# Value stage of a hybrid trunk kernel: the gate-activations are rounded on ScalarE, and the gates lie in device memory in another order

## The reference, cut to what matters

```
q = (x @ w_q).reshape(n, P_HEADS, 2, P_QDIM // 2)
s = jnp.einsum('nhjd,hjkd->nhjk', q, sub_keys).astype(jnp.float32)
sv, si = lax.top_k(s, P_TOPK)
...
gate = jax.nn.softmax(tv, axis=-1).astype(x.dtype)
u = u_tab[eidx]
act = jax.nn.gelu(jnp.einsum('nhkd,nd->nhk', u, x), approximate=False)
return jnp.einsum('nhk,nhkd->nd', gate * act, v_tab[eidx])
```

## Time and profile before

| | us |
|---|---|
| median of 3 runs | 2930.12 |
| lowest, highest run | 2927.99, 2931.79 |
| the profiled execution | 2933.7 |
| span in its profile, first to last instruction | 2931.1 |
| first `v` tile on TensorE, layer 0 and layer 1 | 1112.1, 2459.2 |

### The profile page before, as it was taken

One profiled execution on the slowest core, in us unless ns is written; L12 is line 12 of the kernel. 1 busy time (PEld: TensorE's weight loads), 2 busy tenths in 40 slices (PEclk: granted clock), 3 DMA queues, 4 the chain that ended last, 5 costly groups with the idle time before them and its releaser, 6 DMA issues.

```text
span 2931.1 us, 51716 instructions
## 1 busy us (share of the span) xinstructions
PE 2811.6 (96%) x20358; PEld 2653.3 (91%) x20358; DVE 1930.2 (66%) x4036; ACT 1030.2 (35%) x1440; POOL 996.9 (34%) x695
## 2 busy tenths in 40 slices
PE   7989999999899999999998979999999999999998
PEld 4966558999899999999998868999899999999997
DVE  3876654587683236888886566488685324888886
ACT  4611104333353333323234354333254333233223
POOL 0000000127888722434320000107788742343430
PEclk9999999999999999999999999999999999999999
DMA  7346634777678778999993303587678778999994
GB/s 244 111 145 235 206 108 151 260 212 172 146 216 196 176 199 277 324 321 326 335 313 114 123 21 123 170 271 179 157 194 210 176 180 261 310 328 330 321 326 151
DMA packets 340184, 631.67 MB, mean 216 GB/s; under 512 B 73808, under 2 KB 221392, under 8 KB 337696
## 3 DMA queue, kind: packets, MB, share of 16 engines
q1 hardware_dynamic: 140960, 428.57, 45.4%
q0 software_dynamic: 81024, 99.92, 13.6%
q10 hardware_dynamic: 118016, 100.67, 10.8%
HBM read 533.37 MB, written 95.35 MB: 215 GB/s over the span
## 4 chain that ended last, share of the span: by engine, by line
PE 89%; DVE 5%; DMA 3%; ACT 1%; issue 1%; another core or an unknown queue 0%; ACTq 0%; SPq 0%; DVEq 0%
PE ps L1216 29%; PE ps L616 15%; PE ps L618 15%; PE ps L617 15%; DMA ring<-in_ada 2%; PE ps L1195 1%; PE ps L589 1%; DVE arena L1664 1%; PE ps L726 1%; PE ps L677 1%; DMA arena<-act_dram 1%; PE ps L1168 1%; PE ps L708 1%; PE ps L793 1%; PE ps L853 1%
## 5 line engine op out<-in xcount | busy, mean ns | idle before, releaser
L1664 DVE TENSOR_TENSOR w_lo<-ring,w_hi 128x1024 fp32r<-128x1024 f32 x576 | 702.6, 1222 | 519.4 <-ACT w_hi L1312 503.6
L1216 PE MATMUL ps<-ga_parts,w_hi 128*128 128x320 f32 x4096 | 901.7, 309 | 3.0 <-DVE ga_parts L1664 3.0
L616 PE MATMUL ps<-hT_hi,w_hi 128*128 128x384 f32 x2576 | 869.2, 337 | 9.5 <-ACT arena L1588 8.1
L617 PE MATMUL ps<-hT_lo,w_hi 128*128 128x384 f32 x2576 | 862.5, 335 | 2.4 <-issue 2.4
L618 PE MATMUL ps<-hT_hi,w_lo 128*128 128x384 f32 x2384 | 798.5, 335 | 2.0 <-issue 2.0
L1312 ACT ACTIVATE w_hi<-ring 128x1024 fp32r<-128x1024 f32 x378 | 400.1, 1060 | 960.3 <-PE ps L618 772.6
L1216 PEld LDWEIGHTS ps<-ga_parts,w_hi 128*128 128x128 f32 x4096 | 684.6, 188 | 3.8 <-issue 2.5
L1216 PE MATMUL ps<-ga_parts,w_lo 128*128 128x320 f32 x2048 | 632.2, 309 | 0.0
L616 PEld LDWEIGHTS ps<-hT_hi,w_hi 128*128 128x128 f32 x2576 | 485.0, 188 | 13.4 <-issue 12.9
L617 PEld LDWEIGHTS ps<-hT_lo,w_hi 128*128 128x128 f32 x2576 | 485.2, 188 | 3.7 <-issue 3.2
L618 PEld LDWEIGHTS ps<-hT_hi,w_lo 128*128 128x128 f32 x2384 | 448.9, 188 | 2.7 <-issue 2.7
(11 more groups left out here) (347 smaller groups left out, 2382.7 us busy)
## 6 DMA issues: line engine op xcount, KB each, us to landing
ring<-in_u SPq DMA_DIRECT2D x256, 512.0 KB
ring<-in_v SPq DMA_DIRECT2D x256, 512.0 KB
ring<-in_ada SPq DMA_DIRECT2D x96, 512.0 KB
act_dram<-arena SPq DMA_DIRECT2D x256, 192.0 KB
arena<-g_dram ACTq DMA_DIRECT2D x32, 1280.0 KB
arena<-act_dram ACTq DMA_DIRECT2D x32, 1280.0 KB
g_dram<-arena POOLq DMA_DIRECT2D x24, 1024.0 KB, 24.7
ring<-in_mix_in SPq DMA_DIRECT2D x42, 512.0 KB
```

The source lines that it names most:

```text
L616: pe.matmul(out, hi[:, c, :], hT_hi[:, c, :], start=(c == 0), stop=False)
L617: pe.matmul(out, hi[:, c, :], hT_lo[:, c, :], start=False, stop=False)
L1216: mm = pe.matmul(ps[:, c, 0:DENSE], l_[:, cs], r_, start=(first and q == 0), stop=(last and q == 2))
L1664: return dve.tensor_tensor(out, a, b, op)
```

## The change

1. VectorE no longer makes the rounded part of `ga`. ScalarE does, in the new `round_in(j, r)`: when tile j-2 is multiplied and the product of tile j is there, it copies `ga` into `ga_parts` with rounding. `round_in(0)` and `round_in(1)` stand ahead of the loop, behind the wait for `act_stored`; in the loop `round_in` of tile j+2 stands ahead of `high_in` of tile j+4.
2. `g_dram` becomes `[i, group of 8 columns, block of 16 tokens, column in the group, token in the block]`, without the first 64 tokens. One `gtile` is then 10,240 consecutive bytes for each i, where it was 20 runs of 512 B. `store_block` writes 16 runs of 512 B for each i, where it wrote 8 KB in one. Zeroing is 16 DMAs of 6 KB for each i, where it was 12 of 8 KB. The addresses for the scatter need the column number's upper and lower bits apart, which adds three operations of VectorE in each of token tiles 0 and 1 (`place_in_g`).

```diff
+DBLK = DENSE // GBLK
+G_ROW, G_JUMP = NJ * DENSE, (DENSE - GBLK) * GJ
...
-        g_dram = nc.dram_tensor("g_dram", [NBLK, P, P, GBLK], F32).ap()
+        g_dram = nc.dram_tensor("g_dram", [P, NJ // GJ, DBLK, GJ, GBLK], F32).ap()
...
                 def store_block(b, blk):
-                    act.dma_start(g_dram[blk].rearrange("i j t -> i (j t)"),
-                                  gstage[:, b].rearrange("p j t -> p (j t)")).then_inc(g_stored[b], 16)
+                    act.dma_start(g_dram[:, :, blk - GATHERED // GBLK].rearrange("i g j t -> i g (j t)"),
+                                  gstage[:, b].rearrange("p (g j) t -> p g (j t)", j=GJ)).then_inc(g_stored[b], 16)
...
-                    act.dma_start(gtile[:, b], g_dram[GATHERED // GBLK:, :, bass.ds(m * GJ, GJ), :].rearrange("b i j t -> i b (j t)"))\
+                    act.dma_start(gtile[:, b].rearrange("p b x -> p (b x)"), g_dram[:, bass.ds(m, 1)].rearrange("i g b j t -> i (g b j t)"))\
                        .then_inc(g_in[b], 16)
...
+                def round_in(j, r=0):
+
+                    act.wait_ge(multiplied, (g0 + j - 1) + r * 2 * GJ)
+                    act.wait_ge(ga_f32, (NJ * layer + j + 1) + r * 2 * GJ)
+                    act.activation(ga_parts[:, j % 2, 0:DENSE], ga[:, j % 2, :], ACT.Copy).then_inc(ga_high, 1)
+
                 for i in range(ASLOTS):
                     act.wait_ge(act_stored[i], 16 * (NJ * (layer + 1) // ASLOTS))
+                round_in(0)
+                round_in(1)
                 with act.Fori(0, NJ // (2 * GJ) - 1) as r:
                     for b in range(2):
                         for k in range(GJ):
+                            round_in(GJ * b + k + 2, r)
                             high_in(WB + GJ * b + k, r)
                         act.wait_ge(ga_f32, (NJ * layer + GJ * (b + 1)) + r * 2 * GJ)
                         load_tiles(r * 2 + (b + 2), b)
-                for j in range(NJ - 2 * GJ + WB, NJ):
-                    high(g0 + j)
+                for j in range(NJ - 2 * GJ + 2, NJ):
+                    round_in(j)
+                    if j + 2 < NJ:
+                        high(g0 + j + 2)
...
+                def place_in_g(row, col, block):
+
+                    chained(dve.tensor_copy(col_group, col))
+                    dve.tensor_scalar(row, row, float(G_ROW), float(block * GJ * GBLK), ALU.mult, ALU.add)
+                    chained(dve.tensor_scalar(col_group, col_group, 3, None, ALU.logical_shift_right))
+                    chained(dve.scalar_tensor_tensor(col, col, float(GBLK), row, ALU.mult, ALU.add))
+                    chained(dve.tensor_scalar(col, col, sc_tok[:, 3:4], None, ALU.add))
...
-                    dve.wait_ge(multiplied, (g - 1) + r * 2 * GJ)
-                    dve.wait_ge(ga_f32, (n + 1) + r * 2 * GJ)
-                    dve.tensor_copy(ga_parts[:, k % 2, 0:DENSE], ga[:, k % 2, :]).then_inc(ga_high, 1)
                     dve.wait_ge(ga_high, (n + 1) + r * 2 * GJ)
...
-                for blk in range(GATHERED // GBLK, 2 * P // GBLK):
-                    pool.dma_start(g_dram[blk].rearrange("i j t -> i (j t)").rearrange("i (r c) -> i r c", c=256), bc(zeros, 1, 8))\
+                for m in range(NJ // GJ):
+                    pool.dma_start(g_dram[:, m, 0:12].rearrange("i b j t -> i (b j t)").rearrange("i (r c) -> i r c", c=256), bc(zeros, 1, 6))\
                         .then_inc(g_zeroed, 16)
```

More of the change, by code:

```diff
@@ L2289, in rank @@
                 chained(dve.reciprocal(gsum[:, 0, :], gsum[:, 0, :]))
+                col_group = gate_rest.bitcast(U32)
+                def place_in_g(row, col, block):
[4 more added lines that the diff above has]
+                    chained(dve.tensor_scalar(col, col, sc_tok[:, 3:4], None, ALU.add))
                 if t == 1:
                     tt(whole_gate.rearrange("p k h -> p h k"), tv, bc(gsum[:, 0, :], 2, TOPK), ALU.mult)
[L2292 to L2295, removed]
+                    row, col = sel3[:, 0, :], sel3[:, 1, :]
+                    place_in_g(row, col, 4)
+                    dve.scalar_tensor_tensor(whole_at.rearrange("p k h -> p (k h)"), col_group, float(G_JUMP), col, ALU.mult, ALU.add)\
+                       .then_inc(scatter_ready, 1)
                     lows(None)
@@ L2303, in rank @@
                     chained(dve.scalar_tensor_tensor(sel3[:, 2, :], col, float(P), row, ALU.mult, ALU.add))
-                    chained(dve.scalar_tensor_tensor(row, row, float(P), col, ALU.mult, ALU.add))
-                    dve.tensor_scalar(row, row, float(GBLK), None, ALU.mult)
+                    place_in_g(row, col, -4)
                     dve.tensor_copy(at[0][near], sel3[near, 2, :])
-                    chained(dve.tensor_scalar(col, sel3[:, 2, :], float(T), None, ALU.mult))
-                    dve.tensor_scalar(at[0][far], row[far], sc_tok[far, 3:4], None, ALU.add)
-                    dve.tensor_scalar(at[1][near], col[near], sc_tok[near, 4:5], None, ALU.add).then_inc(scatter_ready, 1)
+                    dve.scalar_tensor_tensor(at[0][far], col_group[far], float(G_JUMP), col[far], ALU.mult, ALU.add)
+                    chained(dve.tensor_scalar(row, sel3[:, 2, :], float(T), None, ALU.mult))
+                    dve.tensor_scalar(at[1][near], row[near], sc_tok[near, 4:5], None, ALU.add).then_inc(scatter_ready, 1)
                     lows(None)
@@ L2370, in peer @@
                 chained(dve.tensor_scalar(low_part, number, GBLK - 1, None, ALU.bitwise_and))
-                chained(dve.scalar_tensor_tensor(sc_tok[:, 3:4], high_part, float(P * P * GBLK), low_part, ALU.mult, ALU.add))
+                chained(dve.scalar_tensor_tensor(sc_tok[:, 3:4], high_part, float(GJ * GBLK), low_part, ALU.mult, ALU.add))
                 dve.tensor_copy(iota_u, bc(iota[:, 0:LOOK], 2, P))
@@ L2496, in _ @@
                 pool.dma_start(A["out_state"][d], sfin[:, d]).then_inc(outs_done, 16)
-            g_flat = g_dram.rearrange("b i j t -> (b i j t)").unsqueeze(1)
+            g_flat = g_dram.rearrange("i g b j t -> (i g b j t)").unsqueeze(1)
             act_flat = act_dram.rearrange("j i t -> (j i t)").unsqueeze(1)
@@ L2503, in scatter_gates @@
                 pool.wait_ge(zeros_ready, layer + 1)
-                for blk in range(GATHERED // GBLK, 2 * P // GBLK):
-                    pool.dma_start(g_dram[blk].rearrange("i j t -> i (j t)").rearrange("i (r c) -> i r c", c=256), bc(zeros, 1, 8))\
+                for m in range(NJ // GJ):
+                    pool.dma_start(g_dram[:, m, 0:12].rearrange("i b j t -> i (b j t)").rearrange("i (r c) -> i r c", c=256), bc(zeros, 1, 6))\
                         .then_inc(g_zeroed, 16)
-                pool.wait_ge(g_zeroed, 16 * 12 * (layer + 1))
+                pool.wait_ge(g_zeroed, 16 * (NJ // GJ) * (layer + 1))
                 pool.wait_ge(scatter_ready, 2 * layer + 1)
```

## The result

| | before | after |
|---|---|---|
| median of 20 runs each, us | 2922.07 | 2935.70 |
| lowest, highest | 2913.78, 2934.93 | 2928.61, 2945.91 |
| ratio after to before, 95% interval | | 1.0043, 1.0032 to 1.0054 |
| the profiled execution; its span | 2933.7; 2931.1 | 2934.43; 2932.6 |

The change costs 12.6 us (9.4 to 15.8).

What follows compares the result with a forecast made beforehand. It took TensorE to bound the value stage, at 3.52 us a tile. Start +12.1, clock +4.2, gains -0.8 and -1.2, end +0.4 made +14.7 us on 2930.1: 2944.8 us, own range 2937 to 2951, with rivals 2925 to 2962.

Steps and rivals of the forecast that it cites:

- The start: Start of each layer's value stage: TensorE waits while the first rounding stands behind the gelu store's landing, 6.3 and 5.8 us, +12.1.
- The clock: After the pause at each value stage's start TensorE resumes at half clock: twice 2.1, +4.2 us, bounds 0 and 6.8.
- The gains: Shorter second load issue no longer delays a gelu in the `u` stage, -0.8 us; late load at tile 32 in time, -1.2.
- The end: Gap ahead of the last two tiles grows by ScalarE's longer rounding and a hand-over, 0.2 us a layer: +0.4 us.
- The sum: All terms together: 12.1 + 4.2 - 0.8 - 1.2 + 0.4 = +14.7 us.
- Steady state: Value loop: rounding on ScalarE lengthens the chain by 0.2 us, within 2.4 us of slack a tile; cost zero.
- First rival: Value loop: the second load's issue stays slow because of its own 1,024 runs; 33 us excess, 2978 us; chance 0.13.
- Second rival: Scatter phase: changed addresses end TensorE's holes in both layers, 19.5 us come back, 2925 us; chance 0.12.
- Third rival: `u` stage: `gstage` stores in 512 B runs take 10.1 us each instead of 3.3; 2971 to 3025 us; chance 0.07.

Runs made afterwards that it cites:

- e1: The changed kernel with both first roundings ahead of ScalarE's wait for the stored gelus: 2916.97 us, ratio 1.0017 to the kernel before.
- e2: The changed kernel with tile 0's rounding ahead of the last u tile's ScalarE work, tile 1's ahead of the wait for stored gelus: 2912.61 us, ratio 1.0000 to before.
- e4: The changed kernel with the old order of `g_dram`, rounding still on ScalarE: 2952.57 us, ratio 1.0143 to the kernel before.
- e9: The kernel before, with GpSimd waiting for each four of its sixteen indirect scatter writes before issuing the next four: 2911.91 us, ratio 0.9995 to before.
- e5: e4 with the first two roundings placed early as in e2: 2957.71 us, ratio 1.0116 to the kernel before.
- e11: e3 (new order of `g_dram`, rounding on VectorE) with the scatter paced as in e9: 2911.36 us, ratio 0.9993 to the kernel before.
- e3: The kernel before with only the new order of `g_dram`, rounding left on VectorE: 2912.27 us, ratio 1.0000 to before.
- e7: e2 with each ScalarE rounding done twice, the first into memory nobody reads: 2922.48 us, ratio 0.9996 to the kernel before.
- e12: e5 with the load of activations issued ahead of the load of gates: 2914.81 us, ratio 1.0010 to the kernel before.
- e6: The kernel before with the loop's two loads (`gtile`, `atile`) issued in the other order: 2915.7 us, one execution only.

## Why the prediction was right

It said +14.7 us on 2930.1; measured is +12.6 on 2922.1. The 9 us between 2944.8 and 2935.7 are for the most part the three runs of before, which lay 8 us above the median of twenty.

- **The start.** Mechanism, place and both layers as predicted, and undone by moving the rounding alone (e1, e2). The size was off: 9.6 us where 12.1 stood. The term that was too large is the landing: 5.2 and 4.75 us were taken, and it was 3.65 in both layers (1109.20 to 1112.85, and 2453.11 to 2456.78). I had read it from GpSimd's start, which is a later event than the landing. GpSimd's first gathers in after:

```profile
1113.48 1.25 POOL L2577 DMA_INDIRECT arena<-act_dram,arena  x1 [65.15 <-DMA act_dram<-arena]
...
2457.37 1.29 POOL L2577 DMA_INDIRECT arena<-act_dram,arena  x1 [62.50 <-DMA act_dram<-arena]
```

  They start 0.6 us after ScalarE's rounding, which waited for the same store. The rest goes, not strictly, with the order of `g_dram`: GpSimd starts 4.3 to 4.6 us behind the `u` stage's end in the eight kernels with the new order and 4.3 to 5.7 in the six with the old. `e4_round_only`, in which the rounding waits for the store under the old order, has both ends of it: its pauses at the start are 5.75 us in layer 0 and 4.8 in layer 1. What in the old order can delay the store wasn't tried. The rounding took 0.47 us for my 0.43.
- **The clock.** 4.2 us predicted; 4.6 and 5.5 us of work ran at 0.50, which makes 2.3 and 2.7 us, 5.0 in all. The 2.7 is also the difference of the 3,024 matmuls' time.
- **The gains.** The wait for the gelu (0.5 and 0.34 us) isn't in after. At that place TensorE waits 0.1 to 0.5 us in both layers of before, e4 and e9 and in layer 0 of e5, the kernels whose second issue is held, and in none of the others. Neither is the gap at tile 32 in after; it cost 1.2 us, as predicted (before's value stage in layer 0 is 1.1 us longer than in layer 1). But e9 and e11 show that such a gap comes and goes with either layout, and e3 and e11 gained nothing that can be measured. So the 0.8 us have a cause that the traces show; the 1.2 us were one execution's chance, credited to the change.
- **The end.** The wait ahead of the last two tiles went from 1.04 to 1.18 us: 0.3 us for both layers, 0.4 predicted.
- **The sum** by what was measured: 9.6 + 5.0 + 0.3 - 0.8 - 1.2 = 12.9 for the two profiled executions' value stages, against 12.6 (9.4 to 15.8). The predicted 14.7 came so near because only one term was far off: 2.5 us too much at the start, against 0.8 too little for the clock. The bounds that the prediction names add up to 2938 to 2950 us, not 2937 to 2951.
- **Steady state.** Zero, as predicted; e7 shows that 0.47 us more would be zero too. One number in it was wrong without effect: TensorE has to wait when an issue is held over 4.5 us, not over 3.7 (e4). A load is issued while ScalarE still copies the `w_hi` ahead of it, which the earlier trace rows already showed: the issue begins at 1169.26, the copy ends at 1169.53.
- **First rival, the issue stays slow.** False: 0.39 us. Where it does stay slow, in e4, the kernel is 42 us over before; the rival asked for 33 on top of the forecast's 14.7. Near, but by other terms: 13.9 us of pauses in place of 33, and a lowered clock behind them that the rival left out.
- **Second rival, the holes go.** They didn't go with the addresses: after loses 6.6 and 5.2 us in that phase, before 10.6 and 10.9. What the rival missed is that they aren't the kernel's alone: on two of three chips the kernels show none. A comparison of kernels on one chip has them on both sides.
- **Third rival, dear 512 B stores.** The DMA share of 810 to 900 us went from 0.84 to 0.93 at the same 229 and 230 GB/s: 8 us more of DMA time for eight stores, about 1 us each and not 7. TensorE loses nothing by it: in 800 to 895 us both kernels do 790 matmuls. The prediction took runs of 512 B to move at the pace of the others, since queues 1 and 10 carry the same 9.4 MB per percent. But queue 10 mixes runs of three lengths. Singled out in the DMA records, a run of 512 B takes 29.5 ns in before (17 GB/s for one DMA engine) and a run of 10 KB takes 449 ns in after (23 GB/s). So the loads of the gates went from 151 to 115 us of all 16 engines, and the sixteen stores from 43 to 63, 1.2 us more each. Neither shows in the time: e3 has both, and its ratio is 1.0000.

## What to carry to other kernels

A piece of work that is moved to another engine inherits all that stands ahead of it there: look at the start of the stage, not only at the beat of the loop, and put its first instances ahead of waits that they don't need (here that one placement was the whole 12.6 us). Taking load off an engine that doesn't set the pace (here 74 us of VectorE) was worth nothing that could be measured. And where work that others wait for stands behind two loads in one queue, try to issue the one with the most and shortest runs last: what an issue cost its engine here depended on the runs ahead of it, not on its own. The load in second place then landed later (20.5 us after its issue in e12), so see that there is room for that.

## What the runs showed of the hardware

- ScalarE's issue of a DMA with 1,024 runs took 2.7 to 9.7 us with a DMA of 2,560 runs just ahead (before, e4, e5, e9), 0.39 us with 128 runs ahead (after); one with 2,560 runs took 0.47 us with 1,024 ahead (e6).
- ScalarE rounds 128x320 in 0.47 us, as long as its gelu of 128x384 from PSUM takes; VectorE needs 0.33.
- After pauses of 4.8 us, and of 2.6 us too (e1), TensorE resumed at 0.50 of its clock, for some 3 to 5.5 us of work.
- Queue 10 went from 10.8% to 10.1% of the DMA engines' time for the same 100.67 MB, with the gates' loads in runs of 10 KB in place of 512 B and the `gstage` stores the other way round. By single runs, 512 B moved at 17 GB/s for one DMA engine (before) and 10 KB at 23 (after). The Trainium skill ("DMA: Bandwidth & Descriptors", Specifications) has line rate from 512 B up; here the runs of 512 B stayed a quarter below the pace of those of 10 KB, and the measurement decides.
- On one of three chips, sixteen indirect DMAs in a row on GpSimd go with 5 to 12 us of standstill of TensorE a layer (e5 to e7), on two others the same code goes without.
